# Expert stage of a two-block kernel: rows of two pairs gathered at once with features on the partitions, weights loaded as whole 2 MB matrices

## The reference

```python
def hier_moe(h, w_grp, w_exp, w1, w3, w2):
    xt = h.reshape(T, D)                       # T = 512, D = 1024
    grp_logits = xt @ w_grp
    p_g, g_sel = lax.top_k(softmax(grp_logits), 1)
    exp_logits = (xt @ w_exp).reshape(T, N_GROUPS, EXP_PER_GROUP)
    ...
    gate = softmax(top_l) * p_g
    ...
    def expert_block(args):
        xb, e = args
        return (silu(xb @ w1[e]) * (xb @ w3[e])) @ w2[e]
    ...
    return segment_sum(ybuf[dest] * w_s[:, None], tok_s)

# in the block:
    h = rmsnorm(x, g_ffn)
    x = x + hier_moe(h, w_grp, w_exp, w1, w3, w2)
```

## Time and profile before

| | |
|---|---|
| median of 3 runs | 1703.67 us (1703.63 to 1703.76) |
| span of the profiled execution | 1701.9 us |
| TensorE busy, share of the span | 1690.3 us, 99% |
| VectorE, ScalarE busy | 895.4 us, 655.5 us |
| granted TensorE clock | 1.000 of 2.4 GHz |
| moved by DMA | 351.69 MB, 207 GB/s over the span |

### The profile page before, as it was taken

The page is one execution under the profiler, slowest core; times in us unless marked ns, Lnnn a source line. Parts: engine busy times, 40 slices in busy tenths (PEclk is TensorE's granted clock), DMA queues, the critical chain, the costliest instruction groups (busy, mean ns, idle before and its releaser), DMA issues.

```text
span 1701.9 us, 23277 instructions
## 1 busy us (share of the span) xinstructions
PE 1690.3 (99%) x9316; PEld 1225.3 (72%) x9316; DVE 895.4 (53%) x1198; ACT 655.5 (39%) x769; POOL 106.7 (6%) x168
## 2 busy tenths in 40 slices
PE   9999999999999999999999999999999999999998
PEld 7888888875454544445588877778888888888887
DVE  6314337463343342434568656577675544773487
ACT  5333433332121111212366643345542234552465
POOL 3000000000000000000002012211000001100100
PEclk9999999999999999999999999999999999999999
DMA  6332222768999999999541322223353258766874
GB/s 210 100 99 89 85 74 90 300 237 346 421 422 422 422 422 422 422 422 422 208 170 55 99 75 75 75 75 125 100 175 115 95 184 194 166 148 221 195 157 131
DMA packets 103853, 351.69 MB, mean 207 GB/s; under 512 B 9104, under 2 KB 9632, under 8 KB 79200
## 3 DMA queue, kind: packets, MB, share of 16 engines
q1 hardware_dynamic: 91440, 324.37, 50.3%
q0 software_dynamic: 12336, 26.23, 7.8%
HBM read 344.29 MB, written 6.29 MB: 206 GB/s over the span
## 4 chain that ended last, share of the span: by engine, by line
PE 98%; DVE 1%; DMA 0%; ACT 0%; issue 0%; SPq 0%; DVEq 0%; ACTq 0%
PE bank L2743 51%; PE bank L3079 13%; PE bank L3494 9%; PE bank L3092 7%; PE bank L2987 3%; PE bank L3034 3%; PE bank L2768 3%; PE bank L3269 2%; PE bank L3299 1%; PE bank L3322 1%; PE bank L3369 1%; PE bank L3194 0%; PE bank L3402 0%; DMA w_stage<-in_w_in 0%; PE bank L3408 0%; PE bank L3387 0%
## 5 line engine op out<-in xcount | busy, mean ns | idle before, releaser
L2743 PE MATMUL bank<-act_hi,w_hi 128*128 128x512 f32 x992 | 390.1, 393 | 0.0
L2743 PE MATMUL bank<-act_hi,w_lo 128*128 128x512 f32 x992 | 386.3, 389 | 0.0
L2743 PE MATMUL bank<-act_lo,w_hi 128*128 128x512 f32 x992 | 386.2, 389 | 0.0
L1749 DVE TENSOR_TENSOR w_lo<-w_stage,w_hi 128x2048 fp32r<-128x2048 f32 x80 | 183.2, 2290 | 222.2 <-ACT w_hi L1045 222.2
L1045 ACT ACTIVATE w_hi<-w_stage 128x2048 fp32r<-128x2048 f32 x80 | 153.3, 1917 | 243.4 <-PE bank L2743 225.2
L3079 PE MATMUL bank<-ring,xgT 128*64 128x512 f32 x992 | 215.7, 592 | 0.2 <-ACT xgT L1264 0.2
L2743 PEld LDWEIGHTS bank<-act_hi,w_hi 128*128 128x128 f32 x992 | 186.2, 188 | 41.0 <-issue 2.9
L2743 PEld LDWEIGHTS bank<-act_hi,w_lo 128*128 128x128 f32 x992 | 186.2, 188 | 39.2
L2743 PEld LDWEIGHTS bank<-act_lo,w_hi 128*128 128x128 f32 x992 | 186.4, 188 | 37.3
L3079 PEld LDWEIGHTS bank<-ring,xgT 128*64 128x64 f32 x992 | 70.7, 137 | 141.5 <-issue 141.0
L3092 PE MATMUL bank<-ring,gatedT 128*64 128x512 f32 x512 | 113.4, 595 | 0.0
(11 more groups left out here) (487 smaller groups left out, 2320.2 us busy)
## 6 DMA issues: line engine op xcount, KB each, us to landing
ring<-in_w SPq DMA_DIRECT2D x188, 1024.0 KB, 12.4
w_stage<-in_w_in SPq DMA_DIRECT2D x43, 1024.0 KB, 5.0
w_stage<-in_w_ff SPq DMA_DIRECT2D x24, 1024.0 KB, 5.6
b_sum<-in_w_ff POOLq DMA_DIRECT2D x12, 1024.0 KB, 12.6
w_stage<-in_w_out SPq DMA_DIRECT2D x8, 1024.0 KB, 5.0
b_one<-in_w_ff SPq DMA_DIRECT2D x6, 1024.0 KB, 7.8
extra<-in_w SPq DMA_DIRECT2D x4, 1024.0 KB, 8.5
branch_gates<-gate_out POOLq DMA_DIRECT2D x16, 256.0 KB, 3.1
```

The lines of the kernel that those rows point to most:

```text
L1749: dve.tensor_tensor(w_lo[s][:, 0:ktiles, :], w_stage[s][:, 0:ktiles, :], w_hi[s][:, 0:ktiles, :].bitcast(F32), ALU.subtract).then_inc(w_lo ...
L2743: ins = pe.matmul(gb[j][:, :], left, right, start=(kc == 0 and k == 0 and n_pass == 0), stop=(kc == g.chunks - 1 and k == g.ktiles - 1 and ...
```

## The change

`gather` now works on a batch of two pairs at a time (`BATCHES` is 8). The normalized rows are the stationary operand (128 features by 128 tokens) and `sel`, now 256 slots wide, is the moving one; the result has the features on the partitions and needs no turn. ACT copies it straight to `xgT`, which holds the slots of both pairs. The norm before the experts writes its rows in the dealt order (`by_place`), and the router's weights are loaded in the same order. `turn_gathered`, `xg_first`, `xg_next` and the copies to them are gone. DVE makes the selections of a batch in the even pair ahead of it (16 instructions); PE gathers in the odd pair.

The ring has six buffers of 2 MB; a matrix is loaded whole, in rows of 16 KB, and freed when both of its halves, for both experts, have been used. The space reserved for descriptors of POOL's DMAs is set to 8192 bytes, and the kernel's own region grows from 103 to 107 units of 2 KB.

```diff
@@
-        ctx.enter_context(nc.sbuf_tensor("fence", [P, 103 * 512], F32))
+        ctx.enter_context(nc.sbuf_tensor("fence", [P, 107 * 512], F32))
@@
-        ring = [at(f"ring{j}", F + 4 * j, [P, 4, 512]) for j in range(12)]
+        ring = [at(f"ring{m}", F + 8 * m, [P, 8, 512]) for m in range(6)]
-        xgT = at("xgT", 13, [P, KT, P])
-        sel = at("sel", 15, [P, NT, P], F32R)
+        xgT = at("xgT", F + 50, [P, KT, 2 * P])
+        sel = at("sel", 13, [P, NT, 2 * P], F32R)
@@
+        def gather_bank(b, first):
+
+            return ((mb[0], mb[1], gb[2], gb[3]) if first else (mb[0], mb[1], mb[0], mb[1]))[b]
+
+        def by_place(rows, t):
+
+            return rows[:, t, :].rearrange("s (k q) -> s q k", k=KT)
@@ SyncE
+            def matrix_used(n, m):
+
+                if m < 4:
+                    sp.wait_ge(up_done, n * 4 + (2 * (m // 2) + 2))
                 else:
                     sp.wait_ge(down_done, n * 3 + 3)
+            def load_matrix(m, e0):
+
+                w, q = divmod(m, 2)
+                rows = A[("w1", "w3", "w2")[w]][0, ds(e0 + q, 1), :, :].rearrange("e (p k) n -> p (e k n)", p=P)
+                sp.dma_start(ring[m][:, :, :].rearrange("p k n -> p (k n)"), rows).then_inc(ring_in[m], 16)
...
-            sp.dma_start(route_f[:, :, 0:NG], A["w_grp"][0].rearrange("(k p) n -> p k n", p=P))\
+            sp.dma_start(route_f[:, :, 0:NG], A["w_grp"][0].rearrange("(p k) n -> p k n", k=KT))\
...
+            for m in range(2):
+                matrix_used(0, m)
+                load_matrix(m, 4)
+            for m in range(2, 6):
+                matrix_used(0, m)
+                load_matrix(m, 2)
             sp.wait_ge(up_done, 4 + EXTRA // 2)
...
+            for m in range(2, 6):
+                matrix_used(1, m)
+                load_matrix(m, 4)
             with sp.Fori(2, PAIRS - 1) as i:
+                for m in range(6):
+                    matrix_used(i, m)
+                    load_matrix(m, i * 2 + 2)
@@ ScalarE
+                def rows(m, first=False):
+                    for b in range(4):
+                        act.wait_ge(rows_in, m * 4 + (b + 1))
+                        act.activation(xgT[:, 2 * b:2 * b + 2, :],
+                                       gather_bank(b, first)[:, :].rearrange("p (k t) -> p k t", k=2),
                                        ACT.Copy).then_inc(rows_out, 1)
...
-                    if not last:
-                        rows(n + 1)
+                    if following is not None:
+                        rows(batch_number(following, r))
@@ VectorE
+                if n == 1:
+                    by_k = "s (q k) -> s q k"
+                    dve.scalar_tensor_tensor(by_place(xn_at[1], t), x[:, t, :].rearrange(by_k, k=KT), rstd[:, t:t + 1],
+                                             gains[:, :].rearrange(by_k, k=KT), ALU.mult, ALU.mult).then_inc(n_xn, 1)
+                    return
@@
+            def make_sel(m, b):
+
+                if not isinstance(b, int) or b:
+                    dve.wait_ge(rows_in, b * 4)
                 for t in range(NT):
+                    for q in range(2):
+                        dve.tensor_scalar(sel[:, t, q * P:(q + 1) * P], iota_place[:, :], place_in[:, t, col(m * 2 + q)],
+                                          None, ALU.is_equal).then_inc(sel_made, 1)
+                    for q in range(2):
+                        mine = sel[:, t, q * P:(q + 1) * P]
+                        dve.wait_ge(sel_made, b * 16 + 4 * t + q + 1)
+                        dve.scalar_tensor_tensor(mine, iota_place[:, :], place_in[:, NT + t, col(m * 2 + q)],
+                                                 mine.bitcast(F32), ALU.is_equal, ALU.add).then_inc(sel_made, 1)
@@
-                make_sel(0, pair_number(0, r))
-                dve.wait_ge(rows_right, 1 if r is None else r + 1)
-                dve.tensor_copy(by_row(xg_first)[:, 3 * P // 4:P, :],
-                                gb[2][:, 0:256].rearrange("s (q k) -> s q k", k=KT)).then_inc(xg_right, 1)
+                make_sel(0, batch_number(0, r))
@@
+                    if following is not None:
+                        make_sel(following, batch_number(following, r))
                     gate_up_product(n)
+                    if not turned_late:
+                        gatedT_copy(n)
...
                         for u in range(2 * NT):
-                            if u == 5:
+                            if u == 3 and turned_late:
                                 gatedT_copy(n)
@@ TensorE
+                def gather(b, first=False):
+
+                    def picked_rows(part, k, t):
+                        return pe.matmul(gather_bank(k // 2, first)[:, (k % 2) * 2 * P:(k % 2 + 1) * 2 * P],
+                                         part[:, t, k * P:(k + 1) * P], sel[:, t, :],
+                                         start=(part is xn_hi and t == 0 and (k % 2 == 0 or not first)),
+                                         stop=(part is xn_lo and t == NT - 1), skip_group_check=True)
 
                     if first:
...
                         for t in range(NT):
+                            pe.wait_ge(sel_made, b * 16 + 4 * t + 4)
...
+                            for k in range(KT):
+                                picked_rows(xn_hi, k, t)
...
+                        for k in range(KT):
                             for t in range(NT):
+                                ins = picked_rows(xn_lo, k, t)
+                            if k % 2:
+                                ins.then_inc(rows_in, 1)
+                        return
+                    pe.wait_ge(sel_made, b * 16 + 16)
+                    for k in range(KT):
+                        if k in (4, 6):
+                            pe.wait_ge(rows_out, b * 4 + (k // 2 - 1))
+                        for part in (xn_hi, xn_lo):
+                            for t in range(NT):
+                                ins = picked_rows(part, k, t)
+                        if k % 2:
                             ins.then_inc(rows_in, 1)
@@
+                def matrices_in(n, w, ahead):
+
+                    if w == 0 and ahead:
+                        pe.wait_ge(extra_in, 16 * EXTRA)
+                        return
+                    for q in range(2):
+                        if w or isinstance(n, int) and n == 0:
+                            pe.wait_ge(ring_in[2 * w + q], n * 16 + 16)
+                        else:
+                            pe.wait_ge(ring_in[2 * w + q], n * 16)
@@ pair
+                    if following is not None:
+                        gather(batch_number(following, r))
+                    if first or odd:
+                        turn_gated(n)
+                    if first:
+                        pe.wait_ge(valued, 1 if r is None else r * NT + 1)
+                    else:
                         output_cut(n - 1)
                         for u in range(2 * NT):
+                            if odd and u in (3, 4):
+                                pe.wait_ge(rows_out, n * 2 + (u + 2))
+                            elif u == 5 and not odd:
+                                turn_gated(n)
+                            elif u == 7:
+                                pe.wait_ge(moe_added, n * 8 + (3 - 8))
+                            spread(n - 1, u // 2, u % 2, spread_bank(u))
+                        pe.wait_ge(moe_added, n * 8 - 6)
                     pe.wait_ge(gatedT_out, n + 1)
+                    matrices_in(n, 2, ahead)
@@
+                gather(batch_number(0, r), first=True)
                 pair(0, first=True)
+                pair(1, ahead=r is None, odd=1, following=1)
+                with pe.Fori(1, BATCHES - 1) as m:
+                    pair(m * 2)
+                    pair(m * 2 + 1, odd=1, following=m + 1)
+                pair(PAIRS - 2)
                 last_pair()
@@
-    nc = bacc.Bacc("TRN2", target_bir_lowering=False, num_devices=1)
+    nc = bacc.Bacc("TRN2", target_bir_lowering=False, num_devices=1, dynamic_dma_scratch_size=8192)
```

More of the change, by code:

```diff
@@ L1272, in embedding_high, with pair @@
                     act.activation(ple_hi[:, :, :], ple_stage[:, :, :], ACT.Copy).then_inc(p_hi, 1)
-                def pair(i, first=False, last=False):
+                def pair(i, first=False, last=False, following=None):
                     n = pair_number(i, r)
@@ L1293, in pair @@
                                        scale=slot_gate[:, col(i)]).then_inc(y_hi_out, 1)
-                rows(pair_number(0, r), first=True)
+                rows(batch_number(0, r), first=True)
                 pair(0, first=True)
-                with act.Fori(1, PAIRS - 1) as i:
-                    pair(i)
+                pair(1, following=1)
+                with act.Fori(1, BATCHES - 1) as m:
+                    pair(m * 2)
+                    pair(m * 2 + 1, following=m + 1)
+                pair(PAIRS - 2)
                 pair(PAIRS - 1, last=True)
@@ L2193, in last_pair @@
```

(37 more changed lines are left out.)

172 lines of the change are left out of this document (31 added, 141 removed).

## The result

The changed kernel takes 1707.61 us in the median, the kernel before 1703.99 in the same comparison: ratio 1.0022, 95% interval 1.0016 to 1.0028. The forecast was 1699.8 with a range to 1707.5. Sign and size are wrong. The executions also spread more: 1704.7 to 1712.4, against 1703.5 to 1705.5 before. One of the 20 executions of the changed kernel took 3132.44 us at a granted clock of 0.783, the slow state; ratio and spread leave it out, and without it the median is 1707.52.

The account below looks back on a forecast made before the run. PE was taken to bound the expert stage with 5 us of lead, the weight transfers next; the last down starting at 826.3 instead of 830.24 gave 1703.67 - 3.9 = 1699.8 us, range 1692.0 to 1707.5.

Parts of the forecast that it names:

- Pairs 0 and 1: Start of the expert stage: pair 0 takes 24.2 us, pair 1 32.5; pair 1's down ends at 430.0, 3.4 later.
- 39 x 9.786 us: Weight stream for thirteen pairs after pair 2's w2: 381.7 us without a break, last w2 landing at 824.8.
- a start priced at 3.2: Weight transfers after an idle stretch: the first 1 MB lands 5.7 us after issue, 3.2 beyond its 2.49.
- The four strided writes: Scaled rows of the norm before the experts, written transposed by VectorE: 2.2 us each instead of 1.28, at most 2.4.
- the first up: Start of pair 0's up: 373.3 instead of 368.36, from 2.35 us of later logits copy and 2.6 of longer gather.
- The half pair at the end: Last pair, from w3 on: 6.91, 0.43, 3.63 and 0.35 us of small waits, so down starts at 826.3.
- What was costed at nothing: In the pairs, ACT's copies, VectorE's 16 selections and its gatedT copy run hidden under PE's work, at no cost.
- PE's own two pairs: TensorE's work in the expert stage: 57.3 us per two pairs, 28.65 per pair, 0.91 less than before.
- A: Expert-stage transfers: rows of 16 KB run at 422 GB/s like 8 KB ones; +2.1 us, 1705.8; chance 0.22.
- C: Ring between pairs 3 and 15: 16 KB rows hold engines longer, rate drops to 415 GB/s; +8, 1711.9; chance 0.11.
- D: TensorE's clock halves after 1.4 us waits, over half of up, six times: about +29 us, 1733; chance 0.04.
- B: Expert stage: PE binds, at 435 GB/s or more or a cheaper prologue; at most -12.3 us, 1691.3; chance 0.18.

Follow-up runs that it names:

- x9_gather_late: The changed kernel with the batch gather put behind down of the odd pair instead of ahead of it; 1700.90 us, 0.9984 of the kernel before.
- x2_matrices_alone: The kernel before, gather in every pair, with the changed kernel's ring of whole 2 MB matrices in rows of 16 KB; 1703.92 us, ratio 1.0000.
- x7_w2_halves: The changed kernel with only w2 loaded in halves of 1 MB, each freed after its half of down; 1704.40 us, 1.0007 of the kernel before.
- x1_pieces: The changed kernel with every matrix loaded in 1 MB halves in rows of 8 KB, each reloaded once used; 1704.18 us, 1.0002 of the kernel before.
- x5_short_gather: The changed kernel with each later gather cut from 64 passes to 8, rows incomplete, for timing only; 1696.90 us, 0.9963 of the kernel before.
- x3_by_expert: The changed kernel with up and down run through one expert's matrix, then the other's; 1890.21 us, 1.1088 of the kernel before.
- x12_strided_read: x9_gather_late with rows written plainly and the gather reading its stationary operand with a step of 8 features; 1757.81 us, 1.0317 of the kernel before.

## Why the prediction was wrong

**The step that failed** is the last one of "Pairs 0 and 1": "from then on they stream without a break". The sum took 3.2 us of start once and then 39 x 9.786 us in one piece, so that a transfer's start was hidden whenever a slot was free before the queue ended. The 16 engines end up to 3 us apart, and the start is hidden only if the issue comes ahead of the first of them: with 2.2 us (x9_gather_late) nothing was lost, with 1.1 to 1.8 (x2_matrices_alone) the first part of w2 came 0.1 to 0.5 us late, with 1.2 to -0.3 (the changed kernel) 0.4 to 1.8. The ring is one pair deep. When w3 of an odd pair has landed, six matrices are still in the queue (its w2, and w1 and w3 of the next pair), 29.4 us. PE needs 6.91 + 7.68 + 0.43 + 3.63 + 6.92 = 25.6 us from there to the end of down, which frees w2. The forecast's own terms so left 3.8 us for a start priced at 3.2, by the landing of one transfer from rest, and this margin was never written down. In the trace PE took 26.6 us (w3 down at 462.02, the end of down 488.6), and the margin was 3.1 us by the last engine and 0.7 by the first. It cost 6.05 us in the trace, which is the difference between 826.3 and 832.35 (the stream began 0.7 us earlier than forecast and up started 0.6 after the last w3 was down, which cancel). x9_gather_late is the proof, x7_w2_halves and x1_pieces agree. The hole of 1.2 us behind the stage is a second loss in this execution; its cause is open, and the forecast had nothing for it.

**Right, by its own numbers.** The four strided writes took 2.02 to 2.09 us (forecast 2.2), the first selection came 2.14 later than before (2.35 for the logits copy ahead of it) and the first up at 372.25 (373.3):

```profile
345.33 2.06 DVE L1767 SCALAR_TENSOR_TENSOR xn<-x_tm,rstd,gain 128x1024 f32<-128x1024 f32 x1
...
363.34 0.48 DVE L2076 TENSOR_SCALAR sel<-iota_place,place_in 128x128 fp32r<-128x128 f32 x2
```

Pair 0 took 24.1 (24.2), pair 1's down ended at 429.10 (430.0). A pass of the gather costs 0.12. The Trainium skill, "TensorE: Matmul & The Clock Gate" (Back-to-back issue gap), has 262 cycles, about 0.109; the measurement decides. A matrix in rows of 16 KB takes 4.89 us where the queue is never empty (4.893, from a line through rows of 2 and 8 KB). By the 3 cycles a packet of the Trainium skill, "DMA: Bandwidth & Descriptors" (Why small descriptors are slow), an estimate is 4.94; here too the measurement decides. The half pair at the end, w3 to down, took 11.36 (11.32). The waits were at w3 of the odd pairs, as forecast, 10.4 us in all instead of some 8. What was costed at nothing (ACT's copies, the 16 selections, the gatedT copy) stayed hidden: from 440 us on PE waited for nothing but weights. Ahead of pair 0's down it waited 0.88 for the tables.

**Mis-sized, though it did not decide.** PE's own two pairs are 58.15 us (523.46 less the wait of 2.71, less 462.60), not 57.3. The gather takes 7.8 to 7.9 instead of 7.68, and from the end of up to down an even pair takes 4.33 where 4.06 was counted: each change between kinds of passes costs about 0.1. PE is thus only 0.6 us per two pairs faster than the stream's 58.7, and 1.0 faster than before, not 1.8.

**The rivals.** A's rate showed in the mean and was not there: breaks at 428, not 422 throughout. C had the sign and the bound (from 4.943 us per 2 MB, 424.3 GB/s, on the kernel is slower than before); the stage came to 387.70 / 78 = 4.970 us, so its arithmetic held, while its mechanism, long rows that hold an engine, is refuted by x2_matrices_alone and x5_short_gather. D was priced as if half of each up ran at half clock, six times; it comes as 3.4 us and 1.7 us a time, in some executions once or more. B fell. None of the rivals was "w2 is freed too late".

## What to carry to other kernels

A ring's depth has to cover the longest time between two frees, not the mean period: when work of two rounds is bundled into one, look at which slot is freed behind the bundle and issue its load early enough (here 2.2 us before the first engine ran dry, 4.3 before the last, lost nothing), or put the bundle behind the freeing step. Then look at what that moves: x9_gather_late freed w2 in time and delayed w1 once. A mean rate equal to the old one can be a faster rate with holes; look at it in slices. Where an operand needs another order, pay for it where it is written once, not where TensorE loads it 64 times a batch.

## What the runs showed of the hardware that was not expected

- A transfer issued to a queue that runs dry: its parts land as if they had started 1.5 to 1.8 us (the first) and 2.7 to 5.0 us (the last of 16) after its issue, and the first packets behind the break are longer, up to 1.9 us instead of 0.61. The delay of the whole matrix varies from 0.1 to 1.8 us within one execution.
- Plain float32 passes of 512 columns take 0.43 us in one column half; two halves side by side give 0.216 each (x3_by_expert).
- A stationary operand read with a step of 32 bytes loads in 338 ns instead of 192 (x12_strided_read).
- After some waits of 0.6 to 2.7 us, and not after others as long, the granted clock is at half for 3.4 us (once for 6.8), at a price of 1.7 us for each 3.4.
